# A decoder step on one core: projection blocks in pairs of seven products, one count of the search on ScalarE, attention's first rows ahead of the key pages, constants in the load stage

## The reference, cut to what matters

```
h    = rmsnorm(x)                      # load stage; hT has 1024 + 64 + 8 = 1096 columns
proj = h @ w_in                        # 29 blocks of 128 columns: indexer, lora, r k v, attention q k v
scores[t,s] = sum_h w[t,h] * relu(q_idx[t,h] . k_idx[s])
sel  = top_k(scores, 256)              # prompt: 6 tiles of 384..1024 keys; sample: 64 rows of 2112 keys
att  = softmax(q k_sel * scale + bias) v_sel      # sample: keys and values from cache pages
rwkv, gates, merge, MLP, norms         # not changed
```

## Time and profile before

| | us |
|---|---|
| three runs | 2772.24, 2782.27, 2783.66 |
| median | 2782.27 |
| the profiled execution, its own time | 2780.18 |
| span of its trace | 2778.4 |
| TensorE busy | 2487.6 (90%) |
| VectorE busy | 1465.6 (53%) |
| ScalarE busy | 551.4 (20%) |
| POOL busy | 93.0 (3%) |
| mean granted clock | 0.943 |

### The profile page before, as it was taken

One profiled execution on the slowest core, in us unless ns is written; L12 is line 12 of the kernel. 1 busy time (PEld: TensorE's weight loads), 2 busy tenths in 40 slices (PEclk: granted clock), 3 DMA queues, 4 the chain that ended last, 5 costly groups with the idle time before them and its releaser, 6 DMA issues. The chain is left out here.

```text
span 2778.4 us, 52435 instructions
## 1 busy us (share of the span) xinstructions
PE 2487.6 (90%) x21869; PEld 1812.8 (65%) x21869; DVE 1465.6 (53%) x2995; ACT 551.4 (20%) x1170; POOL 93.0 (3%) x133
## 2 busy tenths in 40 slices
PE   6989999957887887887688888999999999999998
PEld 4566666635545555556365566778888888888886
DVE  3348999962371461552456565666543543533543
ACT  3221000121221222222254453212100100100101
POOL 0010000010010010100101110000000000000000
PEclk9989999978998998798799999999999999999999
DMA  5414222151231221320587775421111111111111
GB/s 169 118 30 146 75 79 77 50 161 43 55 104 35 66 81 43 87 66 23 157 271 241 225 260 185 147 76 46 46 31 46 46 31 46 46 38 39 46 31 72
DMA packets 289077, 252.38 MB, mean 91 GB/s; under 512 B 53527, under 2 KB 240505, under 8 KB 288718
## 3 DMA queue, kind: packets, MB, share of 16 engines
q1 hardware_dynamic: 208502, 187.67, 22.4%
q10 hardware_dynamic: 80344, 61.41, 7.5%
HBM read 200.43 MB, written 48.59 MB: 90 GB/s over the span
## 5 line engine op out<-in xcount | busy, mean ns | idle before, releaser
L502 PE MATMUL first_banks<-hT,w_pr 128*128 128x384 f32 (+3 forms) x1392 | 443.5, 480 | 6.0 <-PEq L178 6.0
L502 PEld LDWEIGHTS first_banks<-hT,w_pr 128*128 128x128 f32 (+1 forms) x1392 | 265.2, 192 | 177.9 <-issue 26.0
L989 PE MATMUL rwkv_banks<-h_chunk,w_gate 128*128 128x384 f32 (+1 forms) x768 | 296.9, 532 | 29.2 <-ACT gate_rows L1326 13.3
L2439 DVE TENSOR_TENSOR x<-x,ps_mm 128x272 f32<-128x272 f32 x280 | 121.2, 437 | 307.8 <-PE ps_mm L2406 307.6
L989 PEld LDWEIGHTS rwkv_banks<-h_chunk,w_gate 128*128 128x128 f32 x768 | 155.6, 214 | 124.0 <-issue 56.2
L2406 PE MATMUL ps_mm<-merged_then_hidden,w_mm 128*128 128x272 f32 x960 | 227.1, 393 | 1.6 <-DVE sums_of_right_sides L2659 0.9
L2406 PEld LDWEIGHTS ps_mm<-merged_then_hidden,w_mm 128*128 128x128 f32 x960 | 182.2, 190 | 39.9 <-DVE sums_of_right_sides L2659 1.3
L2430 ACT COPY merged_then_hidden<-ps_mm 128x272 f32<-128x272 f32 x160 | 61.7, 386 | 720.1 <-PE ps_mm L2406 720.1
L2406 PE MATMUL ps_mm<-v_T_and_gates_then_h_mlp,w_mm 128*128 128x272 f32 x864 | 204.5, 392 | 0.0
L2406 PEld LDWEIGHTS ps_mm<-v_T_and_gates_then_h_mlp,w_mm 128*128 128x128 f32 x864 | 164.1, 190 | 33.9
L751 DVE TENSOR_SCALAR_CACHE_REDUCE idx_pages<-scores,mid 128x384 f32<-128x384 f32 (+1 forms) x180 | 170.3, 946 | 6.4
(11 more groups left out here) (443 smaller groups left out, 3634.4 us busy)
## 6 DMA issues: line engine op xcount, KB each, us to landing
k_pages<-in_cache_k SPq DMA_DIRECT2D x128, 256.0 KB, 3.4
v_pages<-in_cache_v SPq DMA_DIRECT2D x128, 256.0 KB, 5.1
w_gate<-in_w_in ACTq DMA_DIRECT2D x48, 512.0 KB, 4.1
w_mm<-in_w_mlp_in SPq DMA_DIRECT2D x32, 512.0 KB, 4.9
w_mm<-in_w_mlp_out SPq DMA_DIRECT2D x32, 512.0 KB, 5.0
w_pr<-in_w_in SPq DMA_DIRECT2D x27, 512.0 KB, 6.0
proj_T<-stage_pr ACTq DMA_DIRECT2D x24, 548.0 KB, 5.7
v_T_and_gates_then_h_mlp<-gates_T SPq DMA_DIRECT2D x16, 544.0 KB, 4.8
```

The source lines that it names most:

```text
L502: ins = MM(B[0:width, 6 + q % 2, 0:m], wk[:, k, 0:width], p.hT[:, k, t0:t0 + m], start=(k == 0), stop=(k == KO - 1))
L989: ins = MM(B[:, GB, 0:w], gw[:, n % 2, k, :], hc[:, k, 0:w], start=(k == 0), stop=(k == KO - 1))
L2439: self.nc.vector.tensor_tensor(to, to, ps, ALU.add).then_inc(self.by_dve, 1)
```

## The change

1. The two blocks on POOL go; the constants and causal masks are made inside load_and_norm, and TensorE waits for the identity.
2. Nine of the 29 blocks are multiplied as before (`DIRECT = 9`); the other 20 make ten pairs (`u`). A pair is seven products (`STEPS`) in two halves of 274 columns, 4 matmuls each: 56 matmuls where there were 48 wider ones. ScalarE copies four of the seven out, VectorE adds the other three. POOL makes four sums of hT once (t1 to t4) and four sums of the weights per pair.
3. The sample's count leaves VectorE: ScalarE does it with a Relu of (score - middle) and a Sign with a sum. VectorE writes `minus` for it and waits for `counted` at the round's end. The 30 rounds are written out, and rounds, finish and additions of the pairs are woven by numbers in which a round is planned at 8.4 and a product at 1.84.
4. In attention `att_v`, `att_k`, `att_q` and the sample's q are loaded ahead of the key pages, three groups of pages follow at once, then masks and the sample's new v; k comes later. TensorE turns the new values later.

```diff
         def _(pool):
+            make_ident(nc, p, pool, const_made)
             nc.gpsimd.memset(eps[:, :], 1e-6).then_inc(eps_set, 1)
+            make_constants(nc, p, pool, const_made)
+            pool.wait_ge(const_made, 6)
+            make_causal_masks(nc, p, pool, neg_made)
+            pool.wait_ge(neg_made, 5)
+            pe.wait_ge(const_made, 2)
...
+DIRECT, ROUNDS = 9, 30
...
+    blocks, pairs = every[0:DIRECT], [every[n:n + 2] for n in range(DIRECT, len(every), 2)]
+    NBK, NPR, W2, KT = len(blocks), len(pairs), NTX // 4, KO // 2
...
+    PAIRS, STEP, SELECT, ROUND, FINISH = 3 * CHUNK * NBK + 0.3, 1.84, 92.0, 8.4, 7.0
+    STEPS, BY_ACT2, BY_DVE2 = ("P1", "P5", "P6", "P2", "P7", "P3", "P4"), ("P1", "P5", "P6", "P4"), ("P2", "P7", "P3")
+    FIRST = {"P2": "P1", "P7": "P5", "P3": "P6"}
...
+    def product(u, step, c):
+        return B[:, {"P2": 2, "P5": 4, "P3": 4}.get(step, 6 * (u % 2)) + c, 0:W2]
...
+            def pair_weights():
+                for u, pair in enumerate(pairs):
+                    yield PAIRS - 3 * CHUNK * (1 - u) if u < 2 else unit_key(u - 1, "P1", 0) + 0.1
+                    if u < 2:
+                        sp.wait_ge(S["made"], 3 * (NBK - 1 + u))
+                    else:
+                        sp.wait_ge(S["u_made"], 14 * (u - 1))
+                    for n, (parts, _, _) in enumerate(pair):
+                        sp.dma_start(w[:, 2 * ((u + 1) % 2) + n, :].rearrange("p (k c) -> p k c", k=KO),
+                                     parts[0][1].rearrange("(k p) c -> p k c", p=128)).then_inc(u_in[u % 2], 16)
+            def pair_rows():
+                for u, pair in enumerate(pairs):
+                    yield unit_key(u + 1, "P1", 0) + 0.8
+                    sp.wait_ge(S["u_act"], 8 * (u + 1))
+                    sp.wait_ge(S["u_dve"], 6 * (u + 1))
...
+            b11, b12, b21, b22 = (p.hT[:, KT * i:KT * i + KT, j * 2 * W2:(j + 1) * 2 * W2] for i in range(2) for j in range(2))
+            pool.wait_ge(S["scores_kept"], 4)
+            pool.wait_ge(S["q_stored"], 32)
+            pool.wait_ge(S["kw_stored"], 16)
+            G.tensor_tensor(t1, b12, b11, ALU.subtract).then_inc(S["t_made"], 1)
+            G.tensor_tensor(t3, b22, b12, ALU.subtract).then_inc(S["t_made"], 1)
+            pool.wait_ge(S["t_made"], 2)
+            G.tensor_tensor(t2, b22, t1, ALU.subtract).then_inc(S["t_made"], 1)
+            pool.wait_ge(S["t_made"], 3)
+            G.tensor_tensor(t4, b21, t2, ALU.subtract).then_inc(S["t_made"], 1)
+            for u in range(NPR):
+                a11, a12, a21, a22, s1, s2, s4 = sides(u)
+                pool.wait_ge(u_in[u % 2], 32 * (u // 2) + 32)
+                if u >= 2:
+                    pool.wait_ge(S["u_made"], 14 * (u - 1))
+                ch.done(G.tensor_tensor(s1, a21, a22, ALU.add))
+                ch.mark(G.tensor_tensor(s2, s1, a11, ALU.subtract))
+                ch.done(G.tensor_tensor(a21, a11, a21, ALU.subtract))
+                G.tensor_tensor(s4, a12, s2, ALU.subtract).then_inc(S["u_summed"], 1)
 
         @block.tensor
         def _(pe):
...
+                for u in range(NPR):
+                    a11, a12, s3, a22, s1, s2, s4 = sides(u)
+                    left = {"P1": a11, "P2": a12, "P3": s4, "P4": a22, "P5": s1, "P6": s2, "P7": s3}
+                    free = {"P1": (u - 2, "P4"), "P5": (u - 1, "P3"), "P6": (u, "P1"), "P2": (u - 1, "P2"),
+                    for step in STEPS:
+                        for c in range(2):
+                            yield unit_key(u, step, c)
+                            if step == "P5" and c == 0:
+                                pe.wait_ge(S["u_summed"], u + 1)
+                                if u == 0:
+                                    pe.wait_ge(S["t_made"], 4)
+                            for k in range(KT):
+                                ins = MM(product(u, step, c), left[step][:, k, :],
+                                         right[step][:, k, c * W2:c * W2 + W2],
+                            ins.then_inc(S["u_made"], 1)
...
+            def keep_pairs():
+                for u in range(NPR):
+                    for step in BY_ACT2:
+                        for c in range(2):
+                            yield unit_key(u, step, c) + STEP + 0.05
+                            act.wait_ge(S["u_made"], made(u, step, c))
+                            nc.scalar.copy(target(u, step, c), product(u, step, c)).then_inc(S["u_act"], 1)
+
+            def count_sample():
+                scratch = ties[0:TS, :]
+                for r in range(ROUNDS):
+                    yield SELECT + ROUND * r + 0.6
+                    act.wait_ge(S["mid_made"], r + 1)
+                    nc.scalar.activation(scratch, p.ss[0:TS, :], ACT.Relu, bias=minus[:, 0:1]).then_inc(S["above_mid"], 1)
+                    yield SELECT + ROUND * r + 2.8
+                    act.wait_ge(S["above_mid"], r + 1)
+                    nc.scalar.activation(scratch, scratch, ACT.Sign, accum_out=cnt[0:TS, nj - 1:nj])\
+                        .then_inc(S["counted"], 1)
...
-            with dve.Fori(0, 30):
-                ch.restart()
-                ch.done(nc.vector.tensor_tensor(mid[:, :], p.lo[:, :], p.hi[:, :], ALU.add))
...
+            def rounds():
+                for r in range(ROUNDS):
+                    yield SELECT + ROUND * r
+                    ch.done(V.tensor_tensor(mid[:, :], p.lo[:, :], p.hi[:, :], ALU.add))
+                    ch.done(V.tensor_scalar(mid[:, :], mid[:, :], 0.5, None, ALU.mult))
+                    V.tensor_scalar(minus[:, 0:1], mid[0:TS, nj - 1:nj], -1.0, None, ALU.mult).then_inc(S["mid_made"], 1)
+                    for n, (j, m, x) in enumerate(tiles[:-1]):
+                        yield SELECT + ROUND * (r + (n + 0.5) / nj)
+                        ch.done(V.tensor_scalar(above[0:m, 0:x.shape[1]], x, mid[0:m, j:j + 1], 0.0, ALU.is_gt, ALU.add,
+                                                accum_out=cnt[0:m, j:j + 1]))
+                    yield SELECT + ROUND * (r + 0.95)
+                    dve.wait_ge(S["counted"], r + 1)
+                    ch.mark(V.tensor_scalar(up[:, :], cnt[:, :], float(TOPK), None, ALU.is_ge))
+                    ch.done(V.tensor_scalar(down[:, :], cnt[:, :], float(TOPK), None, ALU.is_lt))
+                    ch.mark(V.copy_predicated(p.lo[:, :], up[:, :], mid[:, :]))
+                    ch.done(V.copy_predicated(p.hi[:, :], down[:, :], mid[:, :]))
+
...
+            def add_pairs():
+                for u in range(NPR):
+                    for step in BY_DVE2:
+                        for c in range(2):
+                            yield unit_key(u, step, c) + STEP + 0.05
+                            dve.wait_ge(S["u_made"], made(u, step, c))
+                            dve.wait_ge(*emptied(u, FIRST[step], c))
+                            to = target(u, step, c)
+                            V.tensor_tensor(to, to, product(u, step, c), ALU.add).then_inc(S["u_dve"], 1)
+
+            weave(rounds(), finish(), add_pairs())
...
-                    yield 2.11 * i - 0.35
+                    yield 2.11 * i - 0.5
-                    yield 2.11 * i - 0.01
+                    yield 2.11 * i - (0.01 if i else 0.45)
...
                     b, j = divmod(J, NQ)
                     yield b + 0.2 * j - 0.38
+                    if J == 0:
+                        sp.wait_ge(S["ids"], 16)
...
+            def new_rows():
+                for key, dst, blk, name in ((-0.42, qa, B_Q, "new_q"), (0.2, va, B_V, "new_v"), (0.3, ka, B_K, "new_k")):
+                    yield key
+                    sp.dma_start(dst[:, :, :], p.proj[blk:blk + HP, :, TP:NT].rearrange("c p t -> p c t"))\
+                        .then_inc(S[name], 16)
+
             def masks():
                 for b in range(NB):
-                    yield b - 0.03
+                    yield b - 0.03 if b else 0.05
+                    if b == 0:
+                        sp.wait_ge(S["mk_zero"], 1)
...
-            for dst, blk in ((va, B_V), (qa, B_Q), (ka, B_K)):
-                sp.dma_start(dst[:, :, :], p.proj[blk:blk + HP, :, TP:NT].rearrange("c p t -> p c t"))\
-                    .then_inc(S["in"], 16)
-            sp.wait_ge(S["ids"], 16)
-            sp.wait_ge(S["mk_zero"], 1)
-            weave(prompt(), keys(), values(), masks())
+            weave(prompt(), keys(), values(), masks(), new_rows())
...
-            def sample():
-                yield -1.0
-                pe.wait_ge(S["in"], 48)
+            def new_values():
-                pe.wait_ge(S["q_made"], 2)
-                pe.wait_ge(S["pr_zero"], 1)
-                pe.wait_ge(S["vn_made"], 1)
+
+            def sample():
...
             def probs():
-                yield -1.0
+                yield 0.621
...
-            dve.wait_ge(S["in"], 48)
+            dve.wait_ge(S["new_q"], 16)
...
-        p.stage(constants)
+        constants(nc, p)
-            p.stage(causal_masks, first)
```

(1 more changed line is left out.)

241 lines of the change are left out of this document (142 added, 99 removed).

## The result

The changed kernel takes 2754.14 us (median of 2753.19, 2753.39, 2754.88 and 2765.13), the kernel before 2782.97 beside it (2772.24 to 2785.19). The ratio is 0.9917, with a 95% interval of 0.9890 to 0.9945: faster by 15 to 31 us. The forecast was 2759.

The account below looks back on a forecast made before the run. VectorE was taken to set the first large stage's end, TensorE 7.7 us behind. Gains of 12.2 (stage), 3.8 (start) and 5.0 (attention) sum to 21.0 off 2780.2, giving 2759; own range 2752 to 2767.

Parts of the forecast that it names:

- TensorE's pause: Ahead of the pairs in the first large stage: TensorE stands from 226.45 to 235.2, 8.8 us, for a late copy.
- Enough for what is blocked by alternation: Rounds beside the pairs: VectorE has 2.3 us to spare per pair, enough for blocking by POOL's sums except in the finish.
- the finish: End of VectorE's work in the first large stage: POOL's weight sums blocking it there set the end, 3 us.
- The rival of the slower side: First large stage: POOL holds VectorE for all its busy time; 23.4 us later, 2795; decides from about 4.2 per pair; 11%.
- 0.2383 at 274, so 26.7 a pair: TensorE's pairs: 0.2383 us a record at 274 columns, 112 records, 26.7 us a pair; ten pairs save 27.7 us.
- 82% of the pairs: VectorE can't start the finish before TensorE is 82% through the pairs, at 479.4 with free ports.
- TensorE and the last stores (products done at 527) are hidden behind it: End of the first large stage: VectorE ends at 537.7 with free ports, behind TensorE's products and the last stores.
- Two reductions and counts, with one input, I take as free: VectorE beside POOL's sums: one-input reductions and counts aren't held; VectorE waits out POOL's step when reading two SBUF tensors.
- the rounds' tiny two-input steps: VectorE's rounds beside POOL: only these tiny steps are held, 1.2 us of a round of 8.7.
- And lands some 4 us later: Attention's page group 0: one more DMA ahead, landing at 1364.4, where TensorE begins at 1366.40; attention's gain taken as 5.0 us.
- one of the forecast's own signs of being wrong: Attention: the forecast is wrong if TensorE waits for pages there.
- Later in the stage TensorE waits for no page, so the shift is carried to its end: Attention after the first logits: their earlier start, taken as 5.0 us, reaches the stage's end.

Follow-up runs that it names:

- stage_alone: The changed kernel with load_and_norm, its two blocks on POOL and attention as in the kernel before; 2767.68 us, ratio 0.9952.
- w_gated: The changed kernel, but POOL's weight sums of pairs 1 to 9 wait for a round that begins after their weights landed; 2752.19 us, ratio 0.9896.

## Why the prediction was right

The time and the sign were right, and so was the main cost, POOL's sums holding VectorE ahead of the first round. That the sum came within 2 us for the stage is in part luck: two errors of about 7 us cancel in it. The terms:

| term | predicted | measured |
|---|---|---|
| a sum of 2192 elements | 5.25 | 4.81 to 4.86 |
| VectorE's first round, in the changed kernel's time | 228 | 228.14 |
| TensorE's pause | 8.8 | 8.50 |
| clock after it | 1 | 2.5 (26 records in 10.2 us, 7.7 at full clock) |
| pairs' start | 265.3 | 267.49 |
| a pair | 26.7 | 25.85, from one P1 to the next, in most |
| a round with its additions | 8.7 | 8.59 |
| waits for `counted` | 0 | 6.0 |
| finish with additions and holds, from its first cast | 61.3 | 59.5 |
| TensorE's wait in the finish | none | 6.95 |
| last product to next stage | hidden | 8.3, not hidden |
| stage | -12.2 | -13.9 (-14.6 in `stage_alone`) |
| start | -3.8 | -3.8 |
| attention | -5.0 | -3.1 at the first logits here (-2.7 on average), -4.3 (1.5) over the stage |

Five steps failed though the sum held.

"Enough for what is blocked by alternation": in the forecast the rounds were to be paced by TensorE, with the holds hidden in 2.3 us a pair and VectorE waiting for products. The holds were 25.2 us in all, and VectorE waited for no product; `w_gated` starts the finish 6.7 us earlier and takes 4.8 us off R, of which 3 were in the forecast as "the finish". The rival of the slower side, POOL holding VectorE in every pair, was right in kind: three steps of each cluster were held, about 2.8 us a pair. It had priced four sums at full length, 5.7, where its turning point stood at 4.2.

"0.2383 at 274, so 26.7 a pair": 0.2366 us a record is the busy time of a group divided by its count, and the end of each run of 16 overlaps the start of the next. In the kernel before:

```profile
2103.69 3.83 PE L2406 MATMUL ps_mm<-merged_then_hidden,w_mm 128*128 128x272 f32 x16
2107.36 3.83 PE L2406 MATMUL ps_mm<-sums_of_right_sides,w_mm 128*128 128x272 f32 x16
```

From start to start it is 3.67 us for 16, which makes 25.9 a pair of 274 columns. Over 82% of the pairs the error is 7 us. It cancels almost wholly against the holds left out above: the finish was forecast to begin 271.2 us behind the reduction by TensorE's pace, and it began 271.3 behind it (484.22), by VectorE's own work and the holds. That is luck, and the round's 8.59 us for 8.7 is the same luck.

"TensorE and the last stores (products done at 527) are hidden behind it": they were not. TensorE was to have no wait in the pairs and had one of 6.95 us behind the sample's finish, and its last product with two stores behind it ends the stage, 1.46 us behind the last mask where it was 0.48 before.

"Two reductions and counts, with one input, I take as free", and only "the rounds' tiny two-input steps" were to be held: the reductions and counts are free, but L888 and L880, which read one tensor, are held too. The Trainium skill, Advanced Engine Details and Errata, section GPSIMD Details, names a two-port mode beside two inputs; a one-input step of 128x7 held for 1.03 us fits that clause, which I had quoted and not applied. No trace shows in which mode a step ran.

"And lands some 4 us later": the first key pages were to be there 11.0 us behind attention's first DMA, and TensorE turned them at 14.5, after 7.83 us of waiting for them. That is one of the forecast's own signs of being wrong. The first page's DMA was issued at 3.7 us (3.15 before) and landed at 11.5 where it had landed at 8.4, with the longer rows of head pair 0 now ahead of it. The term was 5.0 and measured 2.7 to 4.3. "Later in the stage TensorE waits for no page, so the shift is carried to its end" overlooked the second head pair's wait for `att_k`, 5.97 us at 1453.27, which is not a page; on average the lead passes it unharmed.

Of the 28.8 us between the medians the stage, the start and attention explain 20 to 22. The rest is inside the interval (15 to 31) and no run ties it to anything in the code; the unchanged rwkv stage moves by more than that between executions.

## What to carry to other kernels

Work moved to an idle POOL isn't free: it can hold VectorE's small steps for the whole length of each POOL step, so start it on the semaphore that marks VectorE's long counting step, which is not held. Two engines that end within a few us of each other must be relieved together: of the two halves of this change the count alone gained 4 us of R and the pairs alone lost 37. Ask too what stands behind the last product: here two stores, 8.3 us. And where one stage's total drowns in another's noise, measure from a fixed event inside the stage: here that stretch repeats within 0.01 us in three profiles of the kernel before and within 0.7 in two of the changed stage.

## What the runs showed of the hardware that was not expected

- VectorE's small steps (128x7) and a 128x128 cast were held by POOL for up to 4.72 us. Counts with an accumulated sum (0.60 us at 384 columns to 1.15 at 896), the two reductions (2.35 and 2.33 us beside t1, the same as in the kernel before) and additions with an input in PSUM (0.44 us, ten of them wholly beside POOL's steps in `w_gated`) were not held.
- Long steps with two inputs in SBUF are held too, and POOL is held by them: in `w_gated` a scan over 64x2112 took 5.44 us instead of 4.55, and POOL's step of 1.28 us took 5.40 beside it.
- A one-input POOL step of 128x2192 lasts 5.75 us, longer than the two-input one of 4.86, and holds as well (5.43 and 5.39 us).
- After the pause of 6.95 us TensorE's next 16 records took 6.23 us instead of 3.86; the granted clock was 0.50 from the start of that work to 509.4, then 1.00. Around the end of the pause of 8.50 us it was 0.50 from about 226 to 236, then 1.00.
